# Leaving 14 tokens out of a block's gate, queries and output projection

## What is computed

```
def second_block(x, meta_tokens, ...):
    h = concat([meta_tokens, x])                      # 272 tokens
    proj = rms_norm(h, mix_pre_g) @ w_in
    z, xbc, dt_raw, q, k, v = parts of proj
    y_ssd = ssd_mixer(z, xbc, dt_raw, ...)            # causal; ends with rms_norm(y * silu(z)) per token
    y_sb = rms_norm(stick_breaking_attention(q, k, v))  # query t sees keys s < t
    mix = concat([y_ssd, y_sb]) @ w_out
    h = h + rms_norm(mix, mix_post_g)
    gu = rms_norm(h, ffn_pre_g) @ w_up
    g = causal_dwconv(gu[..., :D_FF], ffn_conv_w, ffn_conv_b)   # 3 taps: token t reads t-2, t-1, t
    f = (gelu(g) * gu[..., D_FF:]) @ w_down
    return (h + rms_norm(f, ffn_post_g))[16:]
```

## Time and profile before

| | us |
|---|---|
| median of 3 runs | 1508.88 |
| lowest, highest | 1502.25, 1509.17 |
| the profiled execution | 1508.11 |
| its span, first to last instruction | 1506.4 |

### The profile page before, as it was taken

The page is one execution under the profiler, slowest core; times in us unless marked ns, Lnnn a source line. Parts: engine busy times, 40 slices in busy tenths (PEclk is TensorE's granted clock), DMA queues, the critical chain, the costliest instruction groups (busy, mean ns, idle before and its releaser), DMA issues.

```text
span 1506.4 us, 15502 instructions
## 1 busy us (share of the span) xinstructions
PE 1368.4 (91%) x6462; PEld 867.2 (58%) x6462; DVE 373.2 (25%) x831; ACT 262.5 (17%) x549; POOL 24.3 (2%) x48
## 2 busy tenths in 40 slices
PE   7988599999979987699999969988899996999997
PEld 6754434444437754444444448866776685888743
DVE  0013322111131332421211140445403304222201
ACT  1012400101111332210100031231234203000000
POOL 3110000000000000000000000000000000000000
PEclk9999599999999987799999979998999998999998
DMA  9951579999962060569999970411131033544420
GB/s 323 314 167 56 196 302 424 428 427 427 405 243 78 1 223 19 214 263 426 427 425 428 410 263 1 166 58 57 56 112 57 0 112 112 168 137 143 167 84 28
DMA packets 89519, 314.33 MB, mean 209 GB/s; under 512 B 7634, under 2 KB 45014, under 8 KB 75622
## 3 DMA queue, kind: packets, MB, share of 16 engines
q1 hardware_dynamic: 77344, 298.98, 51.4%
q10 hardware_dynamic: 12102, 14.30, 3.3%
HBM read 311.03 MB, written 2.24 MB: 208 GB/s over the span
## 4 chain that ended last, share of the span: by engine, by line
PE 88%; DVE 8%; DMA 2%; issue 1%; ACT 1%; DVEq 0%; ACTq 0%; SPq 0%; POOLq 0%
PE psum L240 39%; PE psum L1347 15%; PE psum L1380 7%; PE psum L578 6%; PE psum L2563 5%; PE psum L1392 4%; PE psum L812 2%; PE psum L459 1%; PE psum L759 1%; PE psum L1522 1%; PE psum L1520 1%; DMA ring<-in_a_w_pw 1%; PE psum L2221 1%; DVE x_nat L531 1%; DVE x_nat L529 1%
## 5 line engine op out<-in xcount | busy, mean ns | idle before, releaser
L240 PE MATMUL psum<-xT,ring 128*128 128x256 f32 (+2 forms) x1792 | 412.6, 392 | 8.8 <-POOLq L439 5.2
L240 PEld LDWEIGHTS psum<-xT,ring 128*128 128x128 f32 x1792 | 345.6, 194 | 72.3 <-issue 15.2
L1347 PE MATMUL psum<-ring,arena 128*64 128x512 f32 x768 | 169.6, 594 | 1.7 <-issue 1.7
L1347 PEld LDWEIGHTS psum<-ring,arena 128*64 128x64 f32 x768 | 54.7, 137 | 104.9 <-issue 104.9
L240 PE MATMUL psum<-arena 128*128 128x128 f32 (+4 forms) x684 | 93.7, 294 | 9.7 <-issue 6.5
L240 PEld LDWEIGHTS psum<-arena 128*128 128x128 f32 (+2 forms) x684 | 85.4, 200 | 14.0 <-issue 10.1
L1380 PE MATMUL psum<-ring,arena 128*64 128x512 f32 x384 | 85.0, 595 | 0.0
L1256 DVE TENSOR_TENSOR arena<-psum,arena 64x512 f32<-64x512 f32 x32 | 34.3, 1071 | 193.4 <-ACT arena L1304 193.4
L2563 PE MATMUL psum<-ring,arena 128*128 128x512 f32 x176 | 75.7, 592 | 0.0
L1304 ACT ACTIVATE arena<-psum 64x512 f32<-64x512 f32 x32 | 18.9, 591 | 262.3 <-PE psum L1347 262.3
L1392 PE MATMUL psum<-arena 128*128 128x512 f32 x128 | 59.2, 605 | 1.8 <-DVE arena L1273 1.8
(11 more groups left out here) (314 smaller groups left out, 1253.6 us busy)
## 6 DMA issues: line engine op xcount, KB each, us to landing
ring<-in_moe_w_gate SPq DMA_DIRECT2D x24, 2048.0 KB, 11.5
ring<-in_moe_w_up SPq DMA_DIRECT2D x24, 2048.0 KB, 15.7
ring<-in_moe_w_down SPq DMA_DIRECT2D x24, 2048.0 KB, 15.9
ring<-in_w_in SPq DMA_DIRECT2D x11, 2048.0 KB, 12.7
ring<-in_w_up SPq DMA_DIRECT2D x22, 1024.0 KB, 7.6
arena<-in_moe_w_gate SPq DMA_DIRECT2D x8, 2048.0 KB, 11.6
ring<-in_w_down SPq DMA_DIRECT2D x5, 2048.0 KB, 7.8
ring<-in_a_w_pw SPq DMA_DIRECT2D x8, 1024.0 KB, 11.3
```

What stands on the lines that cost most here:

```text
L240: last = nc.tensor.matmul(dst, lhsT, rhs, start=(n == 0), stop=(n == len(pairs) - 1))
L1347: last = pe.matmul(bank(j)[part, :], tokens[:, k, side * SEATS:side * SEATS + SEATS], weights(u + n, k), start=(k == 0), stop=(k == KC - 1))
```

## The change

`NEED` is 14, the first token that is still needed. Gate, queries, the meta steps of the attention, its norm and the output projection now work on columns 14 to 271 (258 of them). The destination in PSUM begins at column 14 as well. Since the transposes still read whole chunks, `turned_in` first fills columns 0 to 13 of its result with zeros, one more ScalarE instruction for z and one for w_out. Keys, values, xbc and dt keep 272 columns. Shortened to its core (the squares, the meta softplus steps and the copies are narrowed in the same way):

```diff
+NEED = META - (FFN_TAPS - 1)
@@ project_turned
-                        last = nc.tensor.matmul(bank(first + c)[:, 0:L],
+                        last = nc.tensor.matmul(bank(first + c)[:, NEED:L],
                                                 slot_k(part_units[half])[:, k, (c % 4) * P:(c % 4) * P + P],
-                                                src[:, k, :], start=(i == 0 and k == 0),
+                                                src[:, k, NEED:L], start=(i == 0 and k == 0),
                                                 stop=(i == len(parts) - 1 and k == KC - 1))
@@ turned_in
+        nc.scalar.activation(turned[:, :, 0:NEED], ident[:, 0:KC * NEED].rearrange("p (c t) -> p c t", c=KC), ACT.Copy,
+                             scale=0.0)
         for c in range(KC):
             job_ready(nc.scalar, first + c)
-            nc.scalar.activation(turned[:, c, :], bank(first + c)[:, 0:L], function).then_inc(
+            nc.scalar.activation(turned[:, c, NEED:L], bank(first + c)[:, NEED:L], function).then_inc(
@@ qk_products
-        products(psum[:, BANKS + n % 4, 0:L], [(slot_k(u)[:, k, (n % 4) * P:(n % 4) * P + P], xT[:, k, :])
-                                               for k in range(KC)]).then_inc(qk_done, 1)
+        at = NEED if n < KC else 0
+        products(psum[:, BANKS + n % 4, at:L], [(slot_k(u)[:, k, (n % 4) * P:(n % 4) * P + P], xT[:, k, at:L])
+                                                for k in range(KC)]).then_inc(qk_done, 1)
@@ stick_breaking: meta_logits, meta_exponents, meta_values
-                    pe.matmul(zm[32 * i:32 * i + 32, 0:L], k_meta[:, 4 * g + i, :], sqT[:, 4 * g + i, :], start=True,
+                    pe.matmul(zm[32 * i:32 * i + 32, NEED:L], k_meta[:, 4 * g + i, :], sqT[:, 4 * g + i, NEED:L], start=True,
-                pe.matmul(zm[:, 0:L], neg_from_meta[:, :, :].rearrange("p h s -> p (h s)"), soft_meta[:, g, :], start=False, stop=True,
+                pe.matmul(zm[:, NEED:L], neg_from_meta[:, :, :].rearrange("p h s -> p (h s)"), soft_meta[:, g, NEED:L], start=False, stop=True,
-                pe.matmul(psum[:, values_bank("meta", n), 0:L], v_meta[:, g, P * (n % 4):P * (n % 4) + P], w_meta[:, g, :],
+                pe.matmul(psum[:, values_bank("meta", n), NEED:L], v_meta[:, g, P * (n % 4):P * (n % 4) + P], w_meta[:, g, NEED:L],
@@ meta_values_out
-                dve.tensor_copy(soT[:, n, 0:META], src[:, 0:META])
+                dve.tensor_copy(soT[:, n, NEED:META], src[:, NEED:META])
@@ project_out
-            products(psum[:, BANKS, 0:L], [(ones[:, :], sqT[:, c, :]) for c in range(KC)]).then_inc(so_summed, 1)
+            products(psum[:, BANKS, NEED:L], [(ones[:, :], sqT[:, c, NEED:L]) for c in range(KC)]).then_inc(so_summed, 1)
-                ins = dve.scalar_tensor_tensor(sbT[:, c, :], soT[:, c, :], column("sb_norm_g_2", c), rms_b,
+                ins = dve.scalar_tensor_tensor(sbT[:, c, NEED:L], soT[:, c, NEED:L], column("sb_norm_g_2", c), rms_b,
```

More of the change, by code:

```diff
@@ L1790, in qk_products @@
             nc.tensor.wait_ge(qk_out, n - 3)
-        products(psum[:, BANKS + n % 4, 0:L], [(slot_k(u)[:, k, (n % 4) * P:(n % 4) * P + P], xT[:, k, :])
-                                               for k in range(KC)]).then_inc(qk_done, 1)
+        at = NEED if n < KC else 0
+        products(psum[:, BANKS + n % 4, at:L], [(slot_k(u)[:, k, (n % 4) * P:(n % 4) * P + P], xT[:, k, at:L])
+                                                for k in range(KC)]).then_inc(qk_done, 1)
     def qk_copy(n):
         nc.scalar.wait_ge(qk_done, n + 1)
-        dst, scale = (sqT, 0.125) if n < KC else (skT, 1.0)
-        nc.scalar.activation(dst[:, n % KC, :], psum[:, BANKS + n % 4, 0:L], ACT.Copy, scale=scale).then_inc(qk_out, 1)
+        dst, scale, at = (sqT, 0.125, NEED) if n < KC else (skT, 1.0, 0)
+        nc.scalar.activation(dst[:, n % KC, at:L], psum[:, BANKS + n % 4, at:L], ACT.Copy, scale=scale).then_inc(
+            qk_out, 1)
     QK_AT = {"inner": 3, ("rows", 0): 1, ("diag", 0): 1, ("rows", 1): 2, ("diag", 1): 2, ("rows", 2): 2,
@@ L2246, in meta_logits @@
                 for i in range(4):
-                    pe.matmul(zm[32 * i:32 * i + 32, 0:L], k_meta[:, 4 * g + i, :], sqT[:, 4 * g + i, :], start=True,
+                    pe.matmul(zm[32 * i:32 * i + 32, NEED:L], k_meta[:, 4 * g + i, :], sqT[:, 4 * g + i, NEED:L], start=True,
                               stop=True, skip_group_check=True)
-                pe.matmul(zm[:, 0:META], meta_rows, not_before[0:META, 0:META], start=False, stop=True, skip_group_check=True).then_inc(zm_ready, 1)
+                pe.matmul(zm[:, NEED:META], meta_rows, not_before[0:META, NEED:META], start=False, stop=True, skip_group_check=True).then_inc(zm_ready, 1)
             def meta_exponents(g):
@@ L2346, in meta_softplus @@
                 act.wait_ge(zm_ready, g + 1)
-                act_step(act.activation(soft_meta[:, g, :], psum[:, META_BANK, 0:L], ACT.Abs))
-                act_step(act.activation(soft_meta[:, g, :], soft_meta[:, g, :], ACT.Exp, scale=-1.0))
-                act.activation(soft_meta[:, g, :], soft_meta[:, g, :], ACT.Ln, bias=1.0).then_inc(m_ln, 1)
+                act_step(act.activation(soft_meta[:, g, NEED:L], psum[:, META_BANK, NEED:L], ACT.Abs))
+                act_step(act.activation(soft_meta[:, g, NEED:L], soft_meta[:, g, NEED:L], ACT.Exp, scale=-1.0))
+                act.activation(soft_meta[:, g, NEED:L], soft_meta[:, g, NEED:L], ACT.Ln, bias=1.0).then_inc(m_ln, 1)
             def meta_weights(g):
                 act.wait_ge(m_expo_ready, g + 1)
-                act.activation(w_meta[:, g, :], psum[:, META_BANK, 0:L], ACT.Exp).then_inc(m_w_ready, 1)
+                act.activation(w_meta[:, g, NEED:L], psum[:, META_BANK, NEED:L], ACT.Exp).then_inc(m_w_ready, 1)
             def squares_of(c):
                 act.wait_ge(so_ready, VALUES["meta", c] + 1)
-                act.activation(sqT[:, c, :], soT[:, c, :], ACT.Square)
+                act.activation(sqT[:, c, NEED:L], soT[:, c, NEED:L], ACT.Square)
             act.preload_act_table_set("natural_log_exp_and_others")
@@ L2412, in meta_add_positive @@
                 dve.wait_ge(m_ln, g + 1)
-                dve.scalar_tensor_tensor(soft_meta[:, g, :], psum[:, META_BANK, 0:L], 0.0, soft_meta[:, g, :], ALU.max,
+                dve.scalar_tensor_tensor(soft_meta[:, g, NEED:L], psum[:, META_BANK, NEED:L], 0.0, soft_meta[:, g, NEED:L], ALU.max,
                                          ALU.add).then_inc(m_soft_ready, 1)
@@ L2462, in program @@
     sbT = carve(2176, KC, L)
-    rms_b = carve(9650, L)
+    rms_b = carve(9650, L - NEED)
     so_summed, sb_normed = sem("so_summed"), sem("sb_normed")
@@ L2496, in _ @@
             act.wait_ge(so_summed, 1)
-            act.activation(rms_b, psum[:, BANKS, 0:L], ACT.Sqrt, bias=eps_cols[:, 1:2], scale=1.0 / D).then_inc(
+            act.activation(rms_b, psum[:, BANKS, NEED:L], ACT.Sqrt, bias=eps_cols[:, 1:2], scale=1.0 / D).then_inc(
                 std_ready, 1)
```

## The result

The changed kernel took 1494.8 us in the median of 7 runs (1487.25 to 1495.58), against 1508.88 us before: ratio 0.9902, interval 0.9880 to 0.9924. It is 14.1 us faster. The forecast was 1501.7 us, with a range down to 1496: the range missed, and the gain is more than twice the 6.4 us of the sum.

What follows compares the result with a forecast made beforehand. The prediction took TensorE to bound the kernel; 6.12 us from 528 narrowed instructions and 0.3 from the meta part, 6.4 us off 1508.11, gave 1501.7 us. The 8-in-10 range was 1496 to 1506.5 us.

Steps and rivals of the forecast that it cites:

- What bounds the kernel: Whole kernel: TensorE busy 91% of 1506.4 us and 88% of the chain that ended last.
- the unit of the sum: Per matmul instruction on TensorE: 229.2 ns apart at 272 columns, 11.6 ns less for fourteen columns fewer.
- The sum by columns: Second block: 528 instructions x 11.6 ns = 6.12 us, with 0.3 for the meta part 6.4 us less.
- The PSUM start at column 14: Narrowed matmuls' destination: feared extra cost per instruction, break-even near 12 ns on each of 528; chance 0.03.
- The key products' slack: SSD chunk 1: 3.5 us slack before the diagonal step, edit takes 0.4; behind it VectorE waits 7.56 us for TensorE.
- What the clock adds to the sum: Low-clock stretches: about 36 changed instructions run there, saving 0 to 0.4 us more; 0 taken.
- The prediction's own sign of it: Low-clock stretches: granted clock differing by more than a few hundredths would move the total by over a microsecond.
- Rival 1: Low-clock stretches come out shorter: 3.4 us less than the sum, 1498.3 us; chance 0.20.
- Rivals 3 and 4: Weight loads or aligned steps set pace: 1508.1 us, chance 0.05; PSUM start column costs extra per instruction: 1510 to 1630, 0.03.

Runs made afterwards that it cites:

- e3: Kernel before with only queries, meta steps of the attention and its norm on 258 columns, gate and output projection on 272; 1501.06 us, ratio 0.9971.
- e7: Changed kernel with 3 extra matmuls of 258 columns behind the gate products; 1496.76 us.
- e14: Changed kernel with 2 extra matmuls of 258 columns at the end of SSD chunk 2, a last-chunk step cut to 13 of 128 tokens; 1497.33 us, 0.9932.
- e6: Kernel before with 6 extra matmuls of 272 columns at the end of the gate products; 1508.93 us, ratio 1.0001.
- e8: Changed kernel with three short chained ScalarE instructions before the gate products, about 1.3 us of TensorE idling; 1500.71 us, ratio 0.9947.

## Why the prediction was wrong

- What bounds the kernel, and the unit of the sum: right. The distance in the output projection came to 55.68 / 256 = 217.5 ns, 11.7 less, against 11.6.
- The sum by columns: right in each place where the granted clock was the same in both kernels: gate 1.50 (1.48; low for its first 3.6 us in both), output projection 2.99 (2.97), e3's piece of 288 instructions 60.41 (0.56 less). The PSUM start at column 14 cost nothing. The key products' slack was read rightly too: VectorE still waits 7.37 us at the off-diagonal step.
- "What the clock adds to the sum" is the step that failed: "Bounds 0 and 0.4; I take 0". I priced the low clock only on the changed instructions, as if the stretches behind them kept their place in the program. They don't: 7.5 us went from the chain, 1.7 near 980 us, 2.9 in the SSD chunks, 1.4 at the untouched keys and 1.6 at the untouched first logits, about 19 times my upper bound. The prediction's own sign of it came: the clock behind 976 us went from 0.87 (rows 8) to 1.00. Rival 1 named this mechanism, but its size was half the spread of three runs, 3.4 us, and its argument against, that "nothing in the edit shortens an idle gap", is beside the point: the gap's place in time is enough.
- The spread itself could have warned. Of 118 timed executions of the kernel before, 16 took 1496.7 to 1502.3 us and 100 took 1506.6 to 1511.3, with two between, at 1503.5 and 1503.6. The three runs I had were one of the first kind and two of the second. The granted clock was 0.943 to 0.947 in the rarer kind and 0.936 to 0.941 in the usual one, 8 us of lost time. The changed kernel, seen at 1487 to 1497, has the clock of the rarer kind: its median and 6.4 us of columns make 1501.2, a time of that kind.
- The range, 1496 to 1506.5, was therefore too narrow below. Rivals 3 and 4 didn't occur.

What stays open: what ties the clock's falls to the time line, and why before settles in one of two kinds. The runs show that the losses behind an edit change with shifts of 1 to 3 us within the block. But the falls aren't fixed in time from the program's start either. In twelve profiles the clock fell 13.4 to 13.6 us ahead of the gate's start, although that start lay anywhere from 892.95 to 896.32 us; in after, e7 and e14 it was 11.6 to 11.7 us, and the gate there had the full clock.

## What to carry to other kernels

Price an edit in two parts: the work it removes, and the time that TensorE spends at the low clock in all that follows, which a shift of 1 us can change by several times its own size. Read the lost time (length times missing share) of every stretch behind the edit, not only of the instructions edited, and let the range take in two to four of its units to either side. Low clock costs only where TensorE is on the chain, so compare pieces of the chain too. Where the losses follow idle gaps, matmuls of no use in those gaps are a cheap test, and here gave 4 us in two gaps of 10 and 12 us and nothing more in two shorter ones.

## What was not expected of the hardware

Time lost to the granted clock came in units of 1.7 us in all 19 profiles, but for the last stretch, which the program's end cuts off. 2.75 us of extra matmuls in e6 cost 0.3 us, 1.3 us of idling in e8 cost 5.9. The Trainium skill ("TensorE: Matmul & The Clock Gate", part 1) says that the monitor runs free of the program and that the penalty of ramps is under 1% of a usual span. The changes with small shifts agree with the first; the constant 13.4 to 13.6 us ahead of the gate in twelve profiles is no sign of it. The trace disagrees with the second: lost time over the whole span was about 6% (granted clock 0.940), and the clock's part of one edit was 0.5%, more than the edit's own 0.4%.
